# Steps before value products in TensorE's beats of a hybrid decoder layer

## The reference

```python
h = x * (1 + scale1) + shift1
z = h @ w_in                                   # q, k, v, gates, indexer columns
o_A = hgrn2_recurrence(...)                    # 8 heads, 128x128 state
o_B = sparse_attention(...)                    # indexer scores, top-k keys, softmax with T5 bias
x  = LN1(ALPHA * x + gate1 * ((sig(ga) * o_A + sig(gb) * o_B) @ w_out))
h2 = x * (1 + scale2) + shift2
# PEER: q = h2 @ w_q, scores against two sets of 128 sub keys, top 16 of each half,
# top 16 of 256 pairs -> 16 experts for each of 8 heads
act = gelu(einsum('nhed,nd->nhe', u_tab[eid], h2))
ff  = einsum('nhe,nhed->nd', softmax(top) * act, v_tab[eid])
x  = LN2(ALPHA * x + gate2 * ff)
```

## Time and profile before

| | |
|---|---|
| median of 3 runs | 2774.15 us (2759.83 to 2788.44) |
| profiled execution | 2759.98 us, span 2758.2 us |
| TensorE, VectorE | 71% and 53% of the span busy |
| ScalarE, GpSimd | 21% and 26% |
| DMA | 811.06 MB, 294 GB/s over the span |
| TensorE clock granted | 0.82 of full |

### The profile page before, as it was taken

One profiled execution on the slowest core, in us unless ns is written; L12 is line 12 of the kernel. 1 busy time (PEld: TensorE's weight loads), 2 busy tenths in 40 slices (PEclk: granted clock), 3 DMA queues, 4 the chain that ended last, 5 costly groups with the idle time before them and its releaser, 6 DMA issues.

```text
span 2758.2 us, 26157 instructions
## 1 busy us (share of the span) xinstructions
PE 1949.9 (71%) x8208; PEld 1038.0 (38%) x8208; DVE 1454.4 (53%) x2958; ACT 574.2 (21%) x1895; POOL 713.0 (26%) x609
## 2 busy tenths in 40 slices
PE   6799996777588996575575666466663466676866
PEld 2288652455564443252132431133430121353511
DVE  2000002663363537479874696865794399525464
ACT  0001000120111554122242222242121121202131
POOL 0000001220100323433234333335332223224242
PEclk9899998676699998788787887787986678667679
DMA  8722420121575989999999999989997799989997
GB/s 282 279 91 99 166 71 22 38 69 49 188 225 160 398 326 364 418 391 393 367 394 419 387 412 412 373 349 420 393 400 283 270 343 382 372 315 413 361 364 305
DMA packets 222078, 811.06 MB, mean 294 GB/s; under 512 B 29459, under 2 KB 93811, under 8 KB 152036
## 3 DMA queue, kind: packets, MB, share of 16 engines
q0 software_dynamic: 78976, 572.70, 52.1%
q1 hardware_dynamic: 131414, 215.85, 22.6%
q10 hardware_dynamic: 11552, 20.85, 2.6%
HBM read 785.02 MB, written 26.66 MB: 294 GB/s over the span
## 4 chain that ended last, share of the span: by engine, by line
DMA 23%; PE 20%; DVE 14%; issue 8%; SPq 6%; POOL 1%; ACT 1%; ACTq 1%; DVEq 0%; POOLq 0%
DMA uv<-in_peer_uv,eidr 10%; PE PS L1271 6%; PE PS L1224 6%; DMA wr<-in_w_oq 4%; PE PS L1313 3%; DVE uv L1606 3%; SPq L1114 2%; DMA kvr<-in_cache_kt 2%; PE PS L1294 1%; DMA vec<-mod_d 1%; DMA uv<-in_peer_uv,eid 1%; SPq L1120 1%; SPq L1128 1%; PE PS L1364 1%; DMA qbt<-mix_d 1%
## 5 line engine op out<-in xcount | busy, mean ns | idle before, releaser
L1224 PE MATMUL PS<-uv,dg 128*32 128x512 f32 x2176 | 733.8, 757 | 417.0 <-ACT dg L1447 381.7
L1606 DVE CUSTOM_DVE_ANT_0 uv<-uv,h2r 128x1024 f32<-128x1024 f32 x544 | 676.8, 1244 | 479.9 <-DMA uv<-in_peer_uv,eidr 431.1
L1181 POOL DMA_INDIRECT uv<-in_peer_uv,eidr x512 | 576.2, 1125 | 1268.5 <-PE PS L1224 1021.1
L1224 PEld LDWEIGHTS PS<-uv,dg 128*32 128x32 f32 x2176 | 193.3, 128 | 832.2 <-ACT dg L1447 520.3
L1435 ACT ACTIVATE acts<-dots 128x2 f32<-128x2 f32 x272 | 55.3, 203 | 1163.0 <-DVE dots L1606 1140.0
L1313 PEld LDWEIGHTS PS<-h2T,wr 128*128 128x128 f32 x1280 | 165.2, 209 | 63.6 <-issue 59.6
L1271 PE MATMUL PS<-htb,wr 128*128 128x416 f32 x512 | 184.5, 516 | 0.0
L1313 PE MATMUL PS<-h2T,wr 128*128 128x128 f32 (+1 forms) x1280 | 176.4, 295 | 1.1 <-ACT h2T L1522 1.1
L393 PE MATMUL PS<-hT,wb 128*128 128x272 f32 (+1 forms) x672 | 157.1, 397 | 15.8 <-PEq L134 15.8
L1447 ACT ACTIVATE dg<-fold,wts 128x32 f32<-128x32 f32 x544 | 140.9, 305 | 0.0
L393 PEld LDWEIGHTS PS<-hT,wb 128*128 128x128 f32 (+1 forms) x672 | 120.6, 180 | 52.8 <-issue 17.5
(11 more groups left out here) (261 smaller groups left out, 2026.4 us busy)
## 6 DMA issues: line engine op xcount, KB each, us to landing
wr<-in_w_oq SPq DMA_DIRECT2D x120, 512.0 KB, 11.7
wb<-in_w_in SPq DMA_DIRECT2D x15, 2048.0 KB, 7.6
w_ada_b<-in_w_ada SPq DMA_DIRECT2D x12, 2048.0 KB, 7.9
wr<-in_w_late SPq DMA_DIRECT2D x32, 512.0 KB, 4.3
h2r<-h_d ACTq DMA_DIRECT2D x32, 256.0 KB, 10.8
uv<-in_peer_uv,eidr POOLq DMA_INDIRECT x512, 12.9
kvr<-in_cache_kt SPq DMA_DIRECT2D x64, 128.0 KB, 12.0
kvr<-in_cache_v SPq DMA_DIRECT2D x64, 128.0 KB, 7.2
```

The source lines that it names most:

```text
L1181: nc.gpsimd.indirect_dma_start(out=uv[j % RING][:, :], out_offset=None, in_=table, in_offset=bass.IndirectOffsetOnAxis(ids, 0)).then_inc(e ...
L1224: mm = nc.tensor.matmul(PS[ST * g:ST * g + ST, at:at + 512], dg[:, j % DR, :], uv[j % RING][:, D + 512 * half:D + 512 * half + 512], start ...
L1606: c.step(nc.vector.tensor_tensor_reduce(out=uv[j % RING][:, 0:D], in0=uv[j % RING][:, 0:D], in1=h2r[:, q // HT % 2, g % 2, :], scale=1.0, ...
```

## The change

TensorE's order within a beat is turned round: it takes the steps of beat q first and the value products of pair q - 1 second. The sample's transposes ("sflip") get one more wait: they start when both groups' exponentials are done, where they waited for each group's normalised probabilities only. The other engines' programs are the same.

```diff
                 elif kind == "sflip":
+                    pe.wait_ge(s_exp, 2)
                     for g in range(2):
                         pe.wait_ge(s_norm, g + 1)
...
             for q in range(-1, NG + 1):
+                for s in beats[q]:
+                    step(*s)
                 if q >= 1:
                     values(q - 1)
-                for s in beats[q]:
-                    step(*s)
```

## The result

| | before | after |
|---|---|---|
| median, 18 runs each | 2779.09 us | 2790.03 us |
| lowest run | 2759.83 us | 2776.75 us |
| profiled execution | 2759.98 us, span 2758.2 | 2783.56 us, span 2781.8 |
| TensorE clock granted | 0.82 | 0.81 |

What follows compares the result with a forecast made beforehand. A loop of gathers, dot products and value products was taken as the bound, paced by DMA from 1050 to 2100 us. Terms summed to +0.8 us, added to the 2774.15 us median: 2775 us, range 2745 to 2806.

Steps and rivals of the forecast that it cites:

- The late projection: 890 to 1040 us: S(1) fills TensorE's idle time, the last late step ends earlier; -7.0 us, other end 0.
- Attention: Tiles 1 to 3: shorter VectorE waits for logits, -4.0 us; values behind transposes cost one pair in all, +5.4 us.
- Projections, norms and queries: Tiles 1 to 3: values wait longer, but DMA stays saturated with enough gathers queued; 0 us.
- The median landing time of gathers: Sign in the later profile: under 8 us, with DMA gaps in the saturated stretch, would prove the prediction wrong.
- Sample indices, keys and values: 2083 to 2462 us: waits for pages with one pair fewer released; +2.7, +1.0 and +2.7 us.
- Mask, softmax and the added wait: Around 2365 us: the transposes' wait for s_exp costs nothing, since a VectorE result needs the same exponential; 0 us.
- the end: Last sample scores and choice of experts: the count of values in between is equal; 0 us, ends -3.4 and +5.4.
- the steps pay: Rival, whole block: all gains in full and no losses, -25.4 us, 2749 us; chance 0.17.
- does nothing: Rival, whole block: DMA paces the loop and the late gain is lost at qbt's load, 2774 us; chance 0.20.
- held buffers: Rival: waits inside S hold two of nine buffers, DMA runs dry outside the saturated stretch; +33.6 us, 2808 us; chance 0.18.

Runs made afterwards that it cites:

- late_first: Kernel before, with steps ahead of values only in beats 0 to 19 (late projections, first index steps): 2777.93 us, ratio 1.0003.
- att_steps: Kernel before, with steps ahead of values only in the attention beats of tiles 1 to 3: 2780.16 us, ratio 1.0006.
- ring8: Kernel before with 8 gather buffers instead of 9 and nothing else changed: 2787.51 us, ratio 1.0041.
- y_steps: Kernel before, with steps ahead of values only in the output projection beats: 2786.23 us, ratio 1.0021.
- tile_rest: Kernel before, with steps ahead of values only in the prompt's index, norm, transpose and query beats from 20 to 174: 2785.47 us, ratio 1.0026.
- sample_steps: Kernel before, with steps ahead of values only from beat 175 on (the sample's steps): 2780.36 us, ratio 1.0029.

## Why the prediction was right and where it was wrong

The mechanism named is the one found: S(q) first fills TensorE's gaps (146 us fewer waits for weights), and a wait in S then holds two buffers (counted at pairs 24, 76 and 140). The sum of +0.8 us missed the 11.7 us: two gains that did not arrive (-7.0 and -4.0) hid losses that were put too low, so that "slower" was forecast at all is partly luck. Three of the signs named for the profile after did not come: the index step among the late ones before 890 us, the wait for qbt ending 7 us earlier, and the DMA share of 1.00. Two terms carry most of the miss.

**The late projection: -7.0 us forecast, nothing left at pair 24.** The prediction put S(1) whole into the idle gap. Its late step went there, its index step waited 14.83 us for ScalarE. Pairs 0 to 20 gained 5.4 us (two against two), but pair 0 itself starts later: its first dot products begin at 896.5 to 900.1 us in the five traces with late steps first, at 893.6 to 898.1 us in the nine others. Why is open. At pair 24 both stand at 1080.7 us on the mean (start plus the first two rows of the table). The end of 0 that the term carried, "if the load lands when it did", is the one that came true: the first logits start at 1061.6 and 1063.1 us in after, at 1060.3 and 1064.7 in before. The load goes out at 1035.68 and 1038.83 against 1038.97 and 1038.63, so one of the two traces gained 3 us at its issue, and late_first shows one way in which such a gain is lost: the load takes longer. The wrong step is that work brought forward on TensorE brings the landing forward.

**Attention: +1.4 us forecast (-4.0 and +5.4), about +8 by the traces, +1.7 (-5.3 to +8.6) by the timing of att_steps.** The 7.9 us of VectorE's waits for logits went as said, yet their half of -4.0 us is not to be found: in tile 2, pairs 68 to 76 take 42.8 us where the two traces of before have 48.5 and 45.8, and pairs 76 to 80 then 24.3 and 23.7 us where they had 18.2 and 18.8. What VectorE saves, it waits for at the next gather. The held pair cost more than one in all, and each cost more than the 5.4 us of the prediction: that price gives all of the DMA rate to gathers, and where weight chunks share it a pair takes 7.5 us. With the five traces that put steps first in attention against the eight others (ring8 left out), the means are 103.8 against 99.5 us, 127.3 against 125.3 and 159.2 against 157.1: 4.3 + 2.0 + 2.1 = 8.4 us, with the spread of the second and third as large as their difference. Over pairs 24 to 184 without 62 to 68 the five lie 8.4 us above the seven others, and there nothing overlaps (7.8 us with y_steps among the others). The DMA rate from 1050 to 2100 us agrees: 385 to 387 GB/s in those five, 388 to 393 in the eight, 386.4 against 389.4 on the mean, and 0.8% of 1050 us is 8 us. The size at tile 1 and over all tiles is that of att_steps too, where nothing else differs; how it is shared between tiles 2 and 3 is an estimate. So the step that failed is the one that closed the stretch of DMA share 1.00 to any order: the loss lies inside it.

**Projections, norms and queries: 0 forecast.** Here the prediction looked at how late V would be and asked whether DMA minds. It did not see the new waits inside S: 3.2 to 77.3 us for qT, 0 to 35.9 us for `rel` (part of it in the late stretch), 7.1 to 27.2 us for h2. By the traces its answer nearly stands (58 to 62 is longer by 1.4 us, two against two), while the timing of tile_rest puts the part at +7.2 us, 1.9 to 12.5. What else tile_rest loses stays open. The median landing time of gathers is 12.5 us (13.0 before), so the queue did stay deep; this sign, named in the prediction, holds.

**Sample indices, keys and values: +2.7, +1.0, +2.7 us forecast; +1.2, +3.4, -2.9 measured** (184 to 192, 192 to 216, 216 to 236, two against two). In the keys, GpSimd's first gather after the second long wait for pages, and the next wait of VectorE for a gather, which answer to the earlier trace rows:

```profile
2316.99 1.16 POOL L1181 DMA_INDIRECT uv<-in_peer_uv,eidr  x1 [14.57 <-PE PS L1224]
```
```profile
2323.57 1.22 DVE L1607 CUSTOM_DVE_ANT_0 uv<-uv,h2r 128x1024 f32<-128x1024 f32 x1 [1.06 <-DMA uv<-in_peer_uv,eidr]
```

That gather is job 413 where it was 415, one pair lower, as said. There is no slack, as said, and it becomes idle time of VectorE, but 1.06 us of it where up to 8.2 was allowed. The values had the wrong sign. The step that waited 15.03 us for pages now waits 1.51 us, and all waits of this kind fell from 21.0 and 21.5 us to 7.2 and 4.2. Ahead of them stand new waits for `ps_s` (3.34 us) and `pTs` (1.93 us):

```profile
2418.91 7.01 PE L1364 MATMUL PS<-pTs,kvr 128*128 128x16 f32 x32 [1.51 <-DMA kvr<-in_cache_v]
```

The gain need not come from there: in sample_steps the wait is gone too, and 216 to 236 takes 162.5 us (before 162.2 and 164.1). The wait of the index step for its pages did not change (32.62 us against 32.91). In the traces without steps first there 192 to 216 goes from 158.0 to 163.1 us and 216 to 236 from 156.8 to 164.9, so none of these three sizes is firm. The timing of sample_steps (+0.29%, 0.01 to 0.57, or 0.3 to 16 us) leaves room for more than the rows show.

**Mask, softmax and the added wait, and the end: 0 forecast.** No wait of TensorE for `s_exp` shows; the transposes wait 3.34 us for VectorE's `ps_s`, which needs the same exponential, as argued. Pairs 248 to 271 take 116.0 us on the mean in both, and the 7.59 us before the last choice are now 0.36. What that is worth can't be told: the choice starts in the stage from 236 to 248, which varies by 21 us whatever the order.

**The sum from what was measured**: 0 (to pair 24) + 4.9 (24 to 40) + 1.4 (58 to 62) - 0.2 (68 to 88) + 3.2 (128 to 152) + 1.2 + 3.4 - 2.9 + 0 = +11.0 us, two against two. That it lands so near 11.7 is luck: the stages left out count too, +3.8 us from 62 to 68, -8.7 from 236 to 248 and -0.3 from the rest, and with them the mean spans differ by only 5.65 us. So the 11.7 us are shown by the 36 timed runs, and of their place only the 8 us of the tiles. Of the rivals, "the steps pay" is refuted (no stage shows a gain that stays but the values, and that one isn't firm), "does nothing" is excluded by the interval, and "held buffers" had the sign and the mechanism but three times the size: its price of a full pair at every page wait is what the sample's rows do not show.

**The yardstick.** I added the sum to a median of three runs, 2774.15 us; over 18 runs it is 2779.09. So 5 of the 15 us between 2775 and 2790.03 are not the change's.

**The interleaving of loads.** The rule of the Trainium skill that I cited against my own middle value ("DMA: Bandwidth & Descriptors", section "Issuing engines are not separate DMA queues") agrees with what is seen here, at qbt, from the load's issue to the first logits: 22.2 us with 3 gathers issued behind the load, 19.8 to 24.3 us with 4, 20.8 to 26.6 us with 6, 26.2 and 30.6 us with 8, 36.0 us with 10. The spread within one count is as large as a step between counts, so it holds for the ends and not for each gather; gathers already under way when the load goes out are not in the counts. Of the 358 GB/s of the Trainium skill ("DMA: Bandwidth & Descriptors", section "Where 436 GB/s comes from"): every trace here runs above it over the 1050 us, at 385 GB/s or more, so for this kernel, on one core, the measurement decides against that figure.

## What to carry to other kernels

In an in-order queue, putting steps ahead of the work that frees buffers swaps one wait for another: before costing it, list every product of another engine that a step needs from its own beat, because those waits appear only after the swap, and everything that frees a buffer stands behind them. Here those products stood behind the next pair's dot products on their own engine. And price a held buffer at the pace at which gathers land where it is held (3.75 us), not at the full DMA rate (2.7 us). Before counting on a load that is issued earlier, ask how many transfers are let in behind it: at qbt they took back the whole gain. When effects of a few us in 2780 are at stake, take the forecast's base and every stage from several executions, leave out the stages that jump whatever the order, and trust a stage only where the kernels with one order in it stand apart from all others.

## What was unexpected

One execution of one kernel differs from the next by up to 31 us over the shared block, in jumps at fixed places: pairs 62 to 68 take 39 to 41 or 45 to 47 us, and nothing between, in all fourteen traces. What flips it was not tried. And one buffer of nine is worth 0.41% (0.17 to 0.66) though DMA is 98% busy from 1050 to 2100 us even without it: one hundredth of that share is 10.5 us, as much as the whole effect of this change, and the two traces of before (1.00 and 0.99) differ by as much.
